# Two buffer slots of 1 MB for gathered expert rows become one more 2 MB slot for weight tiles, in a two-block transformer kernel

## The reference, cut to what matters

```python
def peer_ffn(h, w_query, sub_keys, expert_u, expert_v):
    q = (t @ w_query).reshape(T, PEER_HEADS, 2, PEER_HALF)
    s = jnp.einsum('thpd,pnd->thpn', q, sub_keys)
    top_s, top_i = lax.top_k(s, PEER_TOPK)            # 16 best keys of each half
    ...                                               # 16 best of 16 x 16 pairs, per head
    act = gelu(einsum('td,ted->te', tb, expert_u[eb]))
    out = einsum('te,ted->td', gb * act, expert_v[eb])
```

## Time and profile before

| | us |
|---|---|
| median of 3 runs | 2465.55 (2462.98 to 2469.85) |
| the profiled execution, its own time | 2464.54 |
| its span, first to last instruction | 2462.7 |
| PE busy | 2161.0 (88%) |
| DVE busy | 1576.9 (64%) |
| POOL busy | 636.5 (26%) |
| ACT busy | 458.7 (19%) |

### The profile page before, as it was taken

How to read it: one execution, slowest core, us unless ns; L and a number is a source line. 1 busy time by engine, 2 the same in 40 slices (tenths; PEclk the granted TensorE clock), 3 DMA queues, 4 the chain that set the end, 5 groups by cost and what they waited for, 6 DMA issues and landing times. The chain is left out here.

```text
span 2462.7 us, 40094 instructions
## 1 busy us (share of the span) xinstructions
PE 2161.0 (88%) x16356; PEld 2003.0 (81%) x16356; DVE 1576.9 (64%) x4201; ACT 458.7 (19%) x986; POOL 636.5 (26%) x518
## 2 busy tenths in 40 slices
PE   9998899777889868788997798878998899999999
PEld 7887789777779868677896786878867798899799
DVE  1259588686778768868787888887688534212310
ACT  2211232101124011112301133100331012101100
POOL 0024334333334333433333313332233200000000
PEclk9999999989989989899998997989989999999999
DMA  8599999999999999999999988999989968568474
GB/s 316 198 387 421 421 421 418 422 421 420 421 418 417 421 411 421 416 422 416 385 421 420 421 350 325 405 424 384 409 332 401 423 240 367 189 240 313 166 257 154
DMA packets 107062, 900.95 MB, mean 366 GB/s; under 512 B 12765, under 2 KB 16897, under 8 KB 18177
## 3 DMA queue, kind: packets, MB, share of 16 engines
q0 software_dynamic: 73904, 537.43, 53.4%
q1 hardware_dynamic: 31872, 357.95, 36.7%
q10 hardware_dynamic: 1104, 3.02, 0.3%
HBM read 897.30 MB, written 1.05 MB: 365 GB/s over the span
## 5 line engine op out<-in xcount | busy, mean ns | idle before, releaser
L2454 POOL DMA_INDIRECT row<-in_experts,idx x448 | 559.1, 1248 | 1189.0 <-DVE acc L2016 552.9
L2033 DVE CUSTOM_DVE_ANT_0 row<-row,h2n 128x1024 f32<-128x1024 f32 x448 | 534.3, 1221 | 161.3 <-DMA row<-in_experts,idx 160.0
L915 PE MATMUL ea<-diag,row 128*128 128x128 f32 x3808 | 492.6, 294 | 137.4 <-DVE diag L2055 137.3
L915 PEld LDWEIGHTS ea<-diag,row 128*128 128x128 f32 x3808 | 481.0, 209 | 150.7 <-DVE diag L2055 149.0
L2016 DVE SCALAR_TENSOR_TENSOR acc<-row,wgt,acc 128x1024 f32<-128x1024 f32 x207 | 265.2, 1281 | 2.0
L1521 ACT ACTIVATE gl<-dots 128x4 f32<-128x4 f32 x128 | 26.3, 206 | 918.5 <-DVE dots L2033 918.4
L997 PE MATMUL pa<-hB,wring 128*128 128x144 f32 (+1 forms) x1056 | 149.5, 306 | 34.9 <-DMA wring<-in_weights 32.2
L997 PEld LDWEIGHTS pa<-hB,wring 128*128 128x128 f32 x1056 | 145.3, 210 | 38.7 <-DMA wring<-in_weights 34.0
L997 PE MATMUL ea<-hB,wring 128*128 128x144 f32 (+1 forms) x1056 | 137.4, 293 | 3.4 <-DMA wring<-in_weights 3.4
L997 PEld LDWEIGHTS ea<-hB,wring 128*128 128x128 f32 x1056 | 135.2, 198 | 4.2 <-DMA wring<-in_weights 3.8
L807 PE MATMUL pa<-hA,wring 128*128 128x128 f32 x960 | 123.1, 281 | 0.0
(11 more groups left out here) (546 smaller groups left out, 3245.7 us busy)
## 6 DMA issues: line engine op xcount, KB each, us to landing
wring<-in_weights SPq DMA_DIRECT2D x110, 2048.0 KB, 11.7
wlate<-in_weights SPq DMA_DIRECT2D x25, 2048.0 KB, 8.3
wring<-in_weights SPq DMA_DIRECT2D x22, 1408.0 KB, 6.6
wlate<-in_weights SPq DMA_DIRECT2D x10, 1408.0 KB, 6.3
more<-in_weights SPq DMA_DIRECT2D x5, 2048.0 KB, 8.3
row<-in_experts,idx POOLq DMA_INDIRECT x448, 18.5
row<-in_weights SPq DMA_DIRECT2D x3, 2048.0 KB, 16.9
wring<-in_weights SPq DMA_DIRECT2D x3, 1792.0 KB, 11.6
```

Source lines behind the costliest of these rows:

```text
L915: m = pe.matmul(EA[c // 4][:, (c % 4) * P:(c % 4 + 1) * P], v[:, c * P:(c + 1) * P], diag[:, DIAG_SLOTS * (q % 2) + i, :], start=False, st ...
L2033: dve.tensor_tensor_reduce(out=r, in0=r, in1=h2n[:, u % 2, :], scale=1.0, scalar=0.0, op0=ALU.mult, op1=ALU.add, accum_out=dots[:, g % 2, ...
L2454: pool.indirect_dma_start(out=expert_rows[slot], out_offset=None, in_=table, in_offset=bass.IndirectOffsetOnAxis(ap=idx[:, k % 3, GB * g + ...
```

## The change

Rows use ten slots from the first to the last gather. The third weight slot `w3` stays in the ring for all 72 tiles of the first model, so tiles 18 to 71 also turn in three slots; the second model's tiles still use two. The first two tiles of the second model now wait for tiles 69 and 70, the former users of their slots. POOL's wait for tile 14 goes. Nothing is computed differently, and no instruction of PE, DVE or ACT other than a buffer's address changes.

```diff
@@ def place1(n)
-    return n % RING if n < TILES1 else n % 2
+    return n % RING if n < UNITS * TILES1 else n % 2
@@ def row_place(n)
-    return n % (ROWS + MORE) if n < LAST_ROWS else (n - LAST_ROWS) % ROWS
+    return n % ROWS
@@ def row_before(n)
-    return n - ROWS - MORE if n < LAST_ROWS + ROWS else n - ROWS
+    return n - ROWS
@@ buffers and semaphores
-        expert_rows = [row[:, i, :] for i in range(ROWS)] + [more[:, i, :] for i in range(MORE)]
+        expert_rows = [row[:, i, :] for i in range(ROWS)]
-        row_full = [sem(f"row_full{i}") for i in range(ROWS + MORE)]
+        row_full = [sem(f"row_full{i}") for i in range(ROWS)]
@@ SP, the second model's tiles
-                    sp.wait_ge(A["a_pj"], (UNITS - 1) * NG + GA[LAST_GROUP[TILES1 - 2 + n]] + 1)
+                    sp.wait_ge(A["a_pj"], (UNITS - 1) * NG + GA[LAST_GROUP[TILES1 - RING + n]] + 1)
@@ POOL, before a gather
-                if ROWS <= n < ROWS + MORE:
-                    pool.wait_ge(A["a_pj"], GA[LAST_GROUP[EARLY1[0] - 1]] + 1)
-                elif ROWS - 2 * len(EARLY1) <= n < ROWS:
+                if ROWS - 2 * len(EARLY1) <= n < ROWS:
```

## The result

| | before | after |
|---|---|---|
| median of 21 runs each, us | 2465.55 (2456.1 to 2469.9) | 2470.80 (2461.0 to 2479.1) |
| ratio, 95% interval | | 1.0026 (1.0015 to 1.0037) |
| the profiled execution, its own time, us | 2464.54 | 2478.09 |
| its span, us | 2462.7 | 2476.3 |
| first dot to unit 2's last dot, us | 1235.8 | 1242.2 |

The kernel became slower by a quarter of one per cent, some 6 us. I had forecast 17 more than before, with 59% for slower by over 0.3%. The time lies in the stated range of 2460 to 2508, but the forecast loss is nearly three times the measured one.

A forecast was written before the change was run, and what follows sets the result against it. The expert stage of units 0 to 2 was taken as bound by bytes. The profiled 2464.5 us plus 17 us for a lower DMA rate, other terms 0, gave 2481.5, forecast as 2482; range 2460 to 2508.

The forecast's parts named there:

- What bounds the kernel: Expert stage of units 0 to 2 is bound by bytes, 418 GB/s; delay of unit 2's last dot delays the end equally.
- The third weight slot adds nothing; PE waits for no tile: In units 0 to 2 the third slot mostly holds a landed tile; earlier arrival worth 0, bounds 5 us either way.
- POOL, SP, the exchange at the stage's start: 0: POOL's changed waits 0 us; SP's earlier second-model tiles 0, bound -4; equal bytes fetched at the stage's start.
- What a slot's turn is made of: Units 0 to 2: 19.9 us landing plus 18.9 us held; with ten slots, gathers must land within 13.4 us.
- The sum in flight, 5.2 to 5.7 MB: Gathers plus tiles in flight in units 0 to 2 fall from 7.2 MB to 5.2, or 5.7 with held time given back.
- The part that was to be given back: Later gathers use up the 1.5 us that landed rows lie waiting, 0.48 slot, keeping up to 5.7 MB in flight.
- The rate at that much in flight, 411 GB/s, and 17 us of it: Units 0 to 2: half-way rate 411 GB/s costs 21 us; four fifths taken, 17 us, chance 0.48.
- The line through two stretches: Between 419 GB/s at 5.5 MB and 372 at 4.5 MB in flight: 5.2 MB gives 404 GB/s, 43 us.
- The first, DMA engines that stay full: Rival for units 0 to 2: four gathers and half a tile keep DMA full; 2465 us, chance 0.28.
- The slot loop: Rival for units 0 to 2: landing stays at 15 us, a slot turns in 33.9; 60 us more, 2524, chance 0.15.
- The seam: Rival around 1380 to 1480 us: one tile fetched earlier saves 5 us and PE's 3.5 us wait; 2456, chance 0.09.

The follow-up runs named there:

- the kernel with ten and two: Ten row slots instead of twelve and two weight slots as before, against the kernel before the change: 2470.31 us, ratio 1.0020.

## Why the prediction was wrong, step by step

- *What bounds the kernel*: right. The stage is bound by bytes (112 us less for 57 MB less), and unit 2's last dot carries its delay on: the second model's first step moved by 7.2 us, the last dot by 6.4.
- *The third weight slot adds nothing; PE waits for no tile*: right, by the kernel with ten and two.
- *POOL, SP, the exchange at the stage's start: 0*: no run contradicts it.
- *What a slot's turn is made of*: right, and it is the cause. With twelve slots a turn is 12 x 1235.8 / 384 = 38.6 us. The means from 200 to 1400 us, worked out row by row from the signals in each trace, in us (in the last column 14.7 to 15.5 are from the dot's start to the release, the rest from there to the issue):

| row slots | turn | issue to landing | landing to dot | dot to next issue |
|---|---|---|---|---|
| 12 | 38.6 | 20.6 | 2.9 | 15.5 |
| 11 | 35.4 | 17.2 | 3.0 | 15.5 |
| 10 (the change) | 32.3 | 14.3 | 2.9 | 15.4 |
| 9 | 29.5 | 12.0 | 2.4 | 15.4 |
| 8 | 28.2 | 10.4 | 2.0 | 16.1 |

  The held time did not shrink, and the time that landed rows lay waiting hardly did. What the lost slots took away came out of the time in flight. The rate held out because the landing time fell almost in step with the number in flight, down to 14.3 us with two slots less.
- *The sum in flight, 5.2 to 5.7 MB*: it came out at the lower end. Counted as in the prediction, the changed kernel has 370 x 13.6 / 1200 = 4.2 gathers in flight, and with the tiles (11.8 us) 5.2 MB. The part that was to be given back by rows waiting less after their landing did not come: 2.9 us before and after.
- *The rate at that much in flight, 411 GB/s, and 17 us of it*: this is the step that failed. The line through two stretches gives 404 GB/s at the 5.2 MB that came, and 43 us. Measured were 415 GB/s and 6 us. The other kernels, counted in the same way, give the scale that the line stood for: 7.2 MB 418 GB/s, 6.2 MB 416, 5.2 MB 415, 4.4 MB 409 and 3.7 MB 383, for twelve slots down to eight. The line gives 367 at 4.4 MB. Its lower end, 372 GB/s at 4.5 MB, was a stretch of the last unit, beside other work; that the engines had been asked for nothing at times is my explanation of it, and not shown. That the forecast was 17 and not 43 is partly luck: I took off half for a part given back that did not come, and a fifth of the rest for the line.
- *An average over the stage*: the second fault in the same step. Taken in steps of a quarter of a microsecond, the changed kernel moves 417 to 422 GB/s when 5 MB or more are in flight, 409 with 4 MB, 390 with 3 and 359 with 2. It has 3 MB or less in flight for 9% of the time, with nine slots it is 25% and with eight 47%, and with twelve next to none. So the loss is made in the low moments, about half of it where PE holds rows longest, and a mean says little about how many of them there are.
- *The rivals.* The first, DMA engines that stay full, was given 0.28 and is nearest: 2465 forecast, 2471 measured, though the 6 us are clear of the noise. The page "DMA: Bandwidth & Descriptors" of the Trainium skill (Anatomy of one DMA) gives a fixed part of some 2.0 us for a transfer. That it lies behind the bytes of a second transfer, and that two slots less would cost 0, was my working from it; that is 6 us off. It does not explain the 118 us of four slots less either. With eight slots nothing at all is in flight for only 0.1% of the time, but 2 MB are for 17% of it, at 328 GB/s, and 3 MB for 27%, at 377. The slot loop, given 0.15 for ten slots, did not set the pace there; with eight it does (118 us, DMA share 0.96). The seam gained nothing.

## What to carry to other kernels

A buffer slot is worth what is left of its turn after the time in which it is held. Work out turn = slots x pace, take off the held part, and compare what is left with the landing time under load. As long as the DMA engines are full even at the moment when slots are held longest, more slots buy nothing; below that point each one costs more than the last (0, 6, 18 and 94 us of stage here, 118 in all). Shortening the hold is worth as much as adding slots, and a deeper ring for a stream that nobody waits for is worth 0. Even where it does end waits (48 us of them beside unit 3), the whole can get slower (by 17 us there), because another stream is then waited for more.

## What the runs showed of the hardware that was not expected

Tiles land in some 12 us beside gathers whether gathers take 19.9 us (twelve slots, tiles 12.1), 16.6 (eleven, tiles 11.9) or 11.3 (nine, tiles 11.7): the backlog of gathers hardly slows them. And two profiles of one kernel, the changed one, differ by 5.4 us in a stretch with the same instructions, with the mean granted clock at 0.89 and 0.90.
